# Attention in a two-block kernel: VectorE takes the maximum of unit t before it normalises unit t-1, and TensorE turns and uses the probabilities one unit later

## The reference

```python
def _fox(qkv, f_logit, q_g, k_g, f_bias):            # 8 heads of 64, causal
    ...
    s = jnp.einsum('bqhd,bkhd->bhqk', qb, k).astype(jnp.float32) * scale
    s = s + cq[..., None] - c[:, :, None, :]         # a bias from the cumulated forget gates
    p = _masked_softmax(s, kpos[None, :] <= t[:, None])
    return jnp.einsum('bhqk,bkhd->bqhd', p.astype(v.dtype), v)
...
def block(args):                                     # _nsa: 8 heads, 2 groups of keys
    ...                                              # o_c over compressed keys, then
    p_s = _masked_softmax(...)                       # selected blocks (at 512 tokens: all of the causal ones)
    p_w = _masked_softmax(s, wmask)                  # window of 512
...
def _memory_xattn(q, mem_kv, q_g, k_g):              # 4 heads of 128 over 256 memory tokens
    p = jax.nn.softmax(s, axis=-1)
```

## Time and profile before

| | before |
|---|---|
| median of 3 runs | 3526.84 us (3525.27 to 3527.54) |
| span of the profiled execution | 3522.9 us |
| PE busy | 3170.9 us (90%) |
| DVE busy | 1387.9 us (39%) |
| ACT busy | 1002.5 us (28%) |
| mean granted TensorE clock | 0.944 |

### The profile page before, as it was taken

One profiled execution on the slowest core, in us unless ns is written; L12 is line 12 of the kernel. 1 busy time (PEld: TensorE's weight loads), 2 busy tenths in 40 slices (PEclk: granted clock), 3 DMA queues, 4 the chain that ended last, 5 costly groups with the idle time before them and its releaser, 6 DMA issues. The chain is left out here.

```text
span 3522.9 us, 64333 instructions
## 1 busy us (share of the span) xinstructions
PE 3170.9 (90%) x25945; PEld 2051.0 (58%) x25946; DVE 1387.9 (39%) x2380; ACT 1002.5 (28%) x1796; POOL 185.3 (5%) x230
## 2 busy tenths in 40 slices
PE   4998888875999999999999979977899899878998
PEld 3888667864333333333333358764688688655786
DVE  5545655665111111111111167345533364546333
ACT  2343432421111111111111123344422223435221
POOL 0000111023000000000000200000000000000000
PEclk8999899986999999999999889988999999979999
DMA  6631222045999999989989733130132232310331
GB/s 229 242 126 32 88 79 86 20 167 181 408 374 409 409 356 375 409 312 409 409 312 410 298 99 96 43 62 25 49 96 96 70 86 84 50 37 1 108 96 59
DMA packets 273128, 642.59 MB, mean 182 GB/s; under 512 B 37066, under 2 KB 97226, under 8 KB 271538
## 3 DMA queue, kind: packets, MB, share of 16 engines
q1 hardware_dynamic: 255794, 601.99, 47.2%
q0 software_dynamic: 6224, 21.24, 1.6%
q10 hardware_dynamic: 10928, 16.79, 1.4%
HBM read 596.68 MB, written 43.27 MB: 182 GB/s over the span
## 5 line engine op out<-in xcount | busy, mean ns | idle before, releaser
L1783 PE MATMUL ps<-raw,ex_xT 128*64 128x512 f32 x3072 | 679.2, 594 | 3.6 <-DMA raw<-in_w_dram 3.6
L1783 PEld LDWEIGHTS ps<-raw,ex_xT 128*64 128x64 f32 x3072 | 218.8, 137 | 418.9 <-issue 409.3
L1882 DVE TENSOR_SCALAR ex_gl<-ps 128x256 f32<-128x256 f32 x96 | 40.8, 425 | 948.7 <-PE ps L1783 948.7
L1783 PE MATMUL ps<-raw,ex_aT 128*64 128x512 f32 x1536 | 349.1, 596 | 2.8 <-DMA raw<-in_w_dram 2.8
L1783 PEld LDWEIGHTS ps<-raw,ex_aT 128*64 128x64 f32 x1536 | 105.6, 137 | 214.1 <-issue 206.5
L2042 PE MATMUL ps<-zlo,hh 128*128 128x512 f32 (+1 forms) x448 | 169.8, 379 | 0.0
L2041 PE MATMUL ps<-zhi,hh 128*128 128x512 f32 (+1 forms) x448 | 168.7, 376 | 1.0 <-DVE hl L2171 0.9
L2043 PE MATMUL ps<-zhi,hl 128*128 128x512 f32 (+1 forms) x448 | 169.0, 377 | 0.0
L2588 PE MATMUL ps<-uu_hi,hh 128*128 128x512 f32 x384 | 151.3, 394 | 10.6 <-DVE uu_lo L2700 10.6
L2590 PE MATMUL ps<-uu_hi,hl 128*128 128x512 f32 x384 | 152.4, 397 | 0.0
L2589 PE MATMUL ps<-uu_lo,hh 128*128 128x512 f32 x384 | 152.3, 397 | 0.0
(11 more groups left out here) (590 smaller groups left out, 5973.0 us busy)
## 6 DMA issues: line engine op xcount, KB each, us to landing
raw<-in_w_dram SPq DMA_DIRECT2D x384, 1024.0 KB, 18.8
oT<-in_w_in_dram SPq DMA_DIRECT2D x64, 512.0 KB, 3.6
u_raw<-in_w_in_dram SPq DMA_DIRECT2D x24, 1024.0 KB, 5.2
expert_out<-xn SPq DMA_DIRECT2D x4, 4096.0 KB, 16.7
expert_out<-ex_yrow ACTq DMA_DIRECT2D x98, 128.0 KB, 5.7
late_ada<-in_w_ada_dram SPq DMA_DIRECT2D x12, 1024.0 KB
early_w<-in_w_in_dram SPq DMA_DIRECT2D x10, 1024.0 KB, 6.7
mT<-in_w_ada_dram SPq DMA_DIRECT2D x3, 2048.0 KB, 18.8
```

The lines of the kernel that those rows point to most:

```text
L1783: mm = pe.matmul(o, x, M["raw"][:, (slot + LATE_SLOTS) % RING, k, h * 512:(h + 1) * 512], start=(s >= 8 and kk == 0), stop=(kk == 7))
```

## The change

Each engine's loop is one step longer. On DVE the maximum of unit t now stands before the normalisation of unit t-1, and the final product comes when t-5 ended a group. On PE the turn in step t is that of unit t-3 and the values those of t-4; on ACT the copy is that of t-3. No instruction is added or removed; each of them has the same operands and the same buffer as before.

```diff
@@ tensor
-            for t in range(n + 3):
+            for t in range(n + 4):
                 if t < n:
                     score(t)
-                if 0 <= t - 2 < n:
-                    turn_probs(t - 2)
-                if t >= 3:
-                    values(t - 3)
+                if 0 <= t - 3 < n:
+                    turn_probs(t - 3)
+                if t >= 4:
+                    values(t - 4)
@@ scalar
-            for t in range(n + 2):
-                if t >= 2:
-                    turned_out(t - 2)
+            for t in range(n + 3):
+                if t >= 3:
+                    turned_out(t - 3)
                 if t < n:
                     exponentials(t)
@@ vector
-            for t in range(n + 4):
+            for t in range(n + 5):
+                if t < n:
+                    maximum(t)
                 if 0 <= t - 1 < n:
                     normalise(t - 1)
-                if t < n:
-                    maximum(t)
-                i = t - 4
+                i = t - 5
                 if i >= 0 and ends[units[i]["out"]] == i:
                     dve.wait_ge(pv, i + 1)
```

## The result

| | before | changed |
|---|---|---|
| median | 3526.06 us, 4 runs (3517.43 to 3527.54) | 3467.32 us, 4 runs (3460.66 to 3468.88) |
| ratio to before, 95% interval | | 0.9835 [0.9823, 0.9847] |
| span of the profiled execution | 3522.9 us | 3465.1 us |
| mean granted clock | 0.944 | 0.945 |

The changed kernel is 58.7 us faster by these medians; 3467.8 us was forecast. That the number fits so closely is partly luck, as the terms show: attention gave 52.6 us where 59 us was forecast.

The account below looks back on a forecast made before the run. The ring of exponentials, normalisation and maximum through DVE's list was taken as the limit. Gains of 33.8 + 1.0 + 11.0 + 7.8 + 7.4 - 2 = 59 us from 3526.8 us gave 3467.8 us, range 3461 to 3482 us.

Parts of the forecast that it names:

- The ring E, N, M: Exponentials on ACT, normalisation and maximum on DVE, each waiting for the one before: 4.13 us a unit at 512 keys.
- nsa groups 2 to 4: Full-clock groups of both nsa layers: 77.32 and 77.34 us go to 60.4 us, gaining 33.8 us.
- PE's need: PE's work alone in an nsa group at full clock, without stalls: 20.14 us of 25.69 us.
- The 2 us held back: Deduction from the summed gains for thin cover in two or three steps of an nsa group; range 0 to 4 us.
- score ring: Score, maximum, exponentials, then score two units on: 3.2 us at 512 keys against 3.7 us of PE work.
- DVE's backlog or the score ring holds on: Rival, 12%: each of 112 units keeps 0.2 us of stall, 22 us of 61 stay, 3488 us.
- First nsa groups and tails: One stall in the first group, 1.0 us; memory units and drains lose all waits, 5.5 us each, 11.0 us.
- 3 us of time at that level: Range allowance: the stages begin at 1.2 GHz and may leave that level 3 us sooner or later.
- Fox stages: Score waits in groups 2 to 4 go, 7.8 us; drains give 3.7 us each, 7.4 us.
- of the stalls about 0.95 us stays: Fox drain: 0.6 us before turns and 0.35 before the last values remain, so each drain gives 3.7 us.
- the falls stay: Rival, 12%: clock falls, three in nsa stages at 1.8 us and both drains at 1.2, cost 8 us: 3476 us.
- slower: Rival, 3%: PE is left at 1.2 GHz; if in all warm nsa groups, 87 us lost against 27 gained, 3587 us.

Follow-up runs that it names:

- The added operations: Changed kernel with each unit's reciprocal on DVE issued twice (0.2 us more a unit), 3470.01 us, or four times (0.6 us more), 3474.44 us.
- the changed kernel again: The changed kernel run a second time with no edit: 3466.82 us.
- the mended drain: Changed kernel with seven unread matmuls ahead of and three behind the transposes before nsa stages, and the last turn but one in another bank pair: 3457.88 us.
- warm starts: Changed kernel with unread matmuls ahead of the nsa stages, in three versions: 3457.72, 3457.88 and 3457.67 us.
- before with a warm start: Kernel before with eight unread matmuls in the stage ahead of each nsa stage: 3523.07 us.
- before with the added operation: Kernel before with each unit's reciprocal on DVE issued twice: 3545.29 us.

## Why the prediction was right, and where it was not

**The cause was right.** The ring E, N, M through DVE's list set the pace. Three things show it: DVE's order alone gives about 41 us, the lag alone none, and 0.2 us in N costs a whole 0.2 us a unit before and nothing in a group after.

**nsa groups 2 to 4, 33.8 us: measured 34.6.** They went from 77.32 and 77.34 to 60.02 and 60.02 us. PE's need worked out from the starts was 20.14 us and is 20.01. The busy time, which the prediction refused as a measure, would have said 20.75. The 2 us held back for thin slack in the score ring weren't needed, and so the rival *DVE's backlog or the score ring holds on* fell. The added operations show the room: nothing was lost at 0.2 us a unit, 0.94 us a group at 0.6.

**First nsa groups and tails, 12.0 us: measured 8.2.** They belong together, since the longer lag carries a turn and values of 384 keys over the mark between groups: less work in the first, more in the tail. From first score to second group and from the last group's end to the next stage it was 22.48 + 34.89 = 57.37 us before in either layer. Now it is 23.06 + 30.17 = 53.23 and 23.11 + 30.16 = 53.27, a gain of 4.1 us in each against 6.5 and 5.5. The tail did what was forecast: no wait of PE's turns or scores for DVE or ACT is left in it, and it is 4.7 us shorter although it holds the carried turn and values. The start didn't: 23.1 us against 22.5, with less work in it. The stage stayed at 0.50 for 20.0 and 20.3 us of its first group, where before it was 13.9 and 15.9 us. The 6.1 and 4.4 us more of it cost up to half, 3.1 and 2.2 us, which is more than what is missing. The prediction had allowed 3 us of time at that level either way and put no price on it. How long it lasts isn't tied to the change in any way that these runs show: the changed kernel again had 20.5 and 16 us, and with one more operation 8.4 us in the first layer (a first group of 17.74 us) and 20.4 in the second.

**Fox stages, 15.2 us: measured 9.7.** The three waits of the earlier trace rows went, and a group takes 10.69 us where 12.06 lay between two of them: about 4 us a stage, as forecast. Two things took 5.5 us back. The larger is the start, which the prediction gave no term of its own, 2.9 us over both layers. Behind the low level PE has new stalls for exponentials, 0.40 and 0.48 us in the first layer and 0.96 in the second, and the low level lasted 6.1 and 8.2 us of these two stages against 5.3 and 7.1 before. The other is the drain, 2.6 us. It gave 2.4 us and not 3.7: before it had stalls of 0.71 + 2.47 us, and its last turn and values, from 2350.42 to 2354.64, ran at 0.63 on the mean; they now take 2.96 us where those took 4.22, 1.3 us less, and the stalls fell by 3.18 - 2.07 = 1.1 us. **The step that failed here is "of the stalls about 0.95 us stays".** PE's timeline has 1.36 + 0.40 + 0.31 = 2.07 us of them in either layer:

```profile
2336.44 0.69 ACT L2398 ACTIVATE za<-ps,fox_nm 128x512 f32<-128x512 f32 x1 [0.84 <-DVE fox_nm L2422]
...
2337.12 0.68 ACT L2398 ACTIVATE za<-ps,fox_nm 128x512 f32<-128x512 f32 x1
...
2337.78 0.59 ACT L2406 ACTIVATE za<-ps 128x512 f32<-128x512 f32 x1
...
2338.52 0.85 PE L2361 MATMUL ps<-small,za 128*128 128x128 f32 x6 [1.36 <-ACT za L2406]
...
2340.36 1.06 PE L2361 MATMUL ps<-small,za 128*128 128x128 f32 x8 [0.40 <-ACT za L2406]
...
2342.54 0.66 PE L2378 MATMUL ps<-za,zb 128*64 128x128 f32 x8 [0.31 <-ACT za L2406]
```

The last turn but one (2338.52) needs the copy of the unit before it. With the new lag that copy, O(13) at 2337.78, stands behind the last two exponentials (2336.44, 2337.12) in ACT's list. The prediction's words on the drain follow M, E and N and PE's work, and not ACT's list. That the wait for this copy is the cause is shown by the mended drain, where the stall of 1.36 us is gone, and 1.27 us with it.

**The number.** Attention gave 52.6 us against 59 forecast, some 11% less: the terms came to 61 with 2 held back. The nsa groups gave 0.8 us more than their term, the starts of the stages fell short by 6.7 us (3.8 nsa, 2.9 fox) and the drains of the fox stages by 2.6. By the stages, 113.3 and 50 to 51 us are longer than the 106 and 48 us that the prediction named, though 106 was counted to an earlier end: by the marks used here the nsa forecast is about 112. That the median hit 3467.8 us all the same is luck: the median of before that the forecast starts from, 3526.8 us, lies 4 to 5 us above those of its later sets. Against these the gain is 55 us.

**The clock.** In the earlier trace rows a group of before has 0.93, and periods of 3.5 us at 0.50 stood inside its groups in both layers. In the changed kernel all groups behind the first show 1.00, in both profiles; so do those of DVE's order alone, and of the changed kernel with added operations and with warm starts. Wherever the ring is closed the falls are there: with the lag alone (2443.5, 2470.5, 3153.5 and 3204.5 us), in before with a warm start, and in before with the added operation, whose three groups of the first layer show 1.00 but whose second layer has one of 0.94 and two of 0.87:

```profile
3188.69:3215.96 27.27, 23.73 (x172) 15.55 (x173) 17.20 (x58) 14.19 (x41) 0.00 (x0) 0.87 0.00 1
```

This group is as long as the one at full clock, 27.27 us, although the clock was low for some 7 us of it: in this group with the ring closed a slower PE cost nothing. So a closed ring doesn't bring a fall each time, but no group behind a first one fell where the ring was open. The rival *the falls stay* fell, and so did *slower*. The Trainium skill, page "TensorE: Matmul & The Clock Gate", section Part 4: PE-mode transpose, says that transposes don't count as busy for that clock in the way other matmuls do. In the nsa groups of the changed kernel the turns are a quarter of PE's time (5.4 of 20 us) and no fall came, so the rule decides nothing there. Ahead of the fox stage the trace is in line with it: the clock fell behind a long row of transposes, and with ordinary matmuls among them it stayed at 1.00. But PE was also less idle there, busy 9.2 of 9.5 us instead of 4.8 of 9.45, and no run here tells the two apart.

**What stays open.** Why the low level at the start of the nsa stage lasts 8 us in one execution and 20 in the next, with PE busy nearly all of it (99% in the first changed profile); and why, once raised ahead of the stage, it fell again with eight matmuls in front and not with seven in front and three behind the transposes.

## What to carry to other kernels

When several engines each run a hand-written loop and all have idle time, follow one unit round the engines and look for an instruction that waits only because its list has another unit's work in front. The length of that closed ring, divided by the units in it, is the pace, and no engine's busy share shows it. An added small operation is a cheap test: if time grows by all of it although the engine is idle, the ring is real.

Here a longer lag paid only once the order had broken the ring, and each step of lag must be walked through the drain on every engine's list, the copies' engine too. And when stalls go, work at the start of a stage that they used to cover begins to cost: here the low clock, 7.5 us a stage, which was worth the next edit (how much of it the stalls had covered before, no run shows). An edit that is to win a few us is priced in the stage that it sits in as well as in the one that it helps: the matmuls ahead of the fox stage cost more than they won.

## What the runs showed of the hardware that was not expected

- The granted clock stayed at 0.50 for 20 us with PE busy 19.74 of 19.96 us, with matmuls of 128 columns in it and transposes. It was at 0.50 and PE waited 9.7 us just ahead of that stage.
- Raised to 1.00 ahead of the stage by eight unread matmuls it fell back 1 to 2 us into it for 17 us (before, both layers), 14 and 6.5 us (changed). With ten around the transposes it held, in both layers and in both kernels that had them.
- Stages that no edit touched differ by up to 10 us in 2300 between executions (the first score at 2290.16 to 2300.17 us), more than several of the terms above. Terms of a few us are read from the stage and not from the median.
